# Small transfers, the last modulation sum and the modulation itself rearranged in a two-layer decoder trunk

## What is computed

```python
cond = jax.nn.silu(c)
mod = (cond @ ada_w[layer] + ada_b[layer])[:, None, :]
sh_m, sc_m, g_m, sh_f, sc_f, g_f = jnp.split(mod, 6, axis=-1)
h = _rmsnorm(x, gn[0]) * (1.0 + sc_m) + sh_m
...
x = x + g_m * _rmsnorm(y, gn[1])
h = _rmsnorm(x, gn[2]) * (1.0 + sc_f) + sh_f
```

## Time and profile before

| | us |
|---|---|
| median of three runs | 901.51 (900.4 to 906.21) |
| profiled execution, its own time | 900.82 |
| its span (first to last instruction) | 899.3 |
| TensorE busy | 837.3 (93%) |
| VectorE busy | 705.9 (78%) |
| ScalarE busy | 524.3 (58%) |
| mean granted TensorE clock | 0.972 of full |

### The profile page before, as it was taken

How to read it: one execution, slowest core, us unless ns; L and a number is a source line. 1 busy time by engine, 2 the same in 40 slices (tenths; PEclk the granted TensorE clock), 3 DMA queues, 4 the chain that set the end, 5 groups by cost and what they waited for, 6 DMA issues and landing times.

```text
span 899.3 us, 12482 instructions
## 1 busy us (share of the span) xinstructions
PE 837.3 (93%) x4720; PEld 741.3 (82%) x4720; DVE 705.9 (78%) x585; ACT 524.3 (58%) x531; POOL 37.9 (4%) x46
## 2 busy tenths in 40 slices
PE   2999999899999999988798899999999999999993
PEld 2999777899999888877677788888888888888882
DVE  4888677876666988553855988898988889898977
ACT  2224924444444434334545678787979787878873
POOL 1001001000000101010000300000000000000120
PEclk9899999899999999689999999999999999999998
DMA  9989867297778998379912799999999999999991
GB/s 341 410 306 377 302 253 286 97 353 262 268 271 300 368 344 322 117 264 420 390 47 61 254 396 343 422 359 419 360 408 360 408 365 406 385 386 393 368 373 47
DMA packets 46239, 283.52 MB, mean 315 GB/s; under 512 B 5855, under 2 KB 5858, under 8 KB 19834
## 3 DMA queue, kind: packets, MB, share of 16 engines
q1 hardware_dynamic: 41002, 268.80, 77.7%
q0 software_dynamic: 3312, 12.06, 3.3%
q10 hardware_dynamic: 1888, 2.15, 0.7%
HBM read 257.82 MB, written 25.17 MB: 315 GB/s over the span
## 4 chain that ended last, share of the span: by engine, by line
PE 81%; DVE 12%; ACT 2%; DMA 2%; issue 2%; ACTq 1%; DVEq 0%; SPq 0%
PE ps L1712 9%; PE ps L1713 9%; PE ps L1717 9%; PE ps L1358 6%; PE ps L1360 6%; PE ps L1361 6%; PE ps L1320 5%; PE ps L1322 5%; PE ps L1321 5%; PE ps L1735 4%; PE ps L1729 4%; PE ps L1730 4%; DVE acc L853 3%; DVE w_lo L837 2%; PE ps L1380 2%; DMA ring<-in_moe_w_down 2%
## 5 line engine op out<-in xcount | busy, mean ns | idle before, releaser
L1169 DVE TENSOR_TENSOR w_lo<-ring,w_hi 128x2048 fp32r<-128x2048 f32 (+1 forms) x96 | 209.7, 2202 | 38.1 <-ACT w_hi L733 36.8
L515 ACT ACTIVATE w_hi<-ring 128x2048 fp32r<-128x2048 f32 (+2 forms) x58 | 109.7, 1893 | 198.0 <-PE ps L1361 100.6
L837 DVE TENSOR_TENSOR w_lo<-ring,w_hi 128x2048 fp32r<-128x2048 f32 (+2 forms) x58 | 138.3, 2385 | 77.1 <-ACT w_hi L515 77.1
L733 ACT ACTIVATE w_hi<-ring 128x2048 fp32r<-128x2048 f32 (+1 forms) x96 | 175.7, 1839 | 20.4 <-PE ps L1717 11.9
L1358 PE MATMUL ps<-hT_lo,w_hi 128*128 128x256 f32 x480 | 137.8, 287 | 4.6 <-DVE hT_lo L876 2.4
L1360 PE MATMUL ps<-hT_hi,w_hi 128*128 128x256 f32 x480 | 136.7, 285 | 0.0
L1361 PE MATMUL ps<-hT_hi,w_lo 128*128 128x256 f32 x480 | 136.7, 285 | 0.0
L853 DVE SCALAR_TENSOR_TENSOR acc<-ring,cond,acc 128x2048 f32<-128x2048 f32 x42 | 98.7, 2349 | 2.7
L1712 PE MATMUL ps<-w_hi,xe_hi 128*128 128x512 f32 (+1 forms) x256 | 97.7, 382 | 2.5 <-DVE xe_lo L1243 2.5
L1358 PEld LDWEIGHTS ps<-hT_lo,w_hi 128*128 128x128 f32 x480 | 93.2, 194 | 5.7 <-issue 2.8
L1169 DVE TENSOR_TENSOR m_lo<-ring,m_hi 128x2048 fp32r<-128x2048 f32 (+2 forms) x48 | 92.7, 1932 | 6.3 <-ACT m_hi L733 6.3
(11 more groups left out here) (289 smaller groups left out, 1442.2 us busy)
## 6 DMA issues: line engine op xcount, KB each, us to landing
ring<-in_moe_w_gu SPq DMA_DIRECT2D x64, 1024.0 KB, 7.1
ring<-in_ada_w SPq DMA_DIRECT2D x48, 1024.0 KB, 6.9
ring<-in_moe_w_down SPq DMA_DIRECT2D x40, 1024.0 KB, 8.3
ring<-in_moe_w_gu SPq DMA_DIRECT2D x32, 768.0 KB, 8.9
ring<-in_ffn_w_gu SPq DMA_DIRECT2D x22, 1024.0 KB, 5.0
ring<-in_sb_w_in SPq DMA_DIRECT2D x12, 1024.0 KB, 7.5
ring<-in_ffn_w_down SPq DMA_DIRECT2D x11, 1024.0 KB, 6.1
x_rows<-blank SPq DMA_DIRECT2D x1, 8704.0 KB, 27.1
```

Of the source, the lines that this page charges most:

```text
L515: act.activation(w_hi[m % 2][:, 0:cols_n], ring[n % R][:, 0:cols_n], ACT.Copy).then_inc(hi_done, 1)
L733: act.activation(m_hi[k % NB][:, 0:n_c], ring[(N0 + k) % R][:, 0:n_c], ACT.Copy).then_inc(hi_done, 1)
L837: dve.tensor_tensor(w_lo[m % 2][:, 0:cols_n], ring[n % R][:, 0:cols_n], w_hi[m % 2][:, 0:cols_n].bitcast(F32), ALU.subtract).then_inc(free ...
L1169: dve.tensor_tensor(m_lo[k % NB][:, 0:n_c], ring[(N0 + k) % R][:, 0:n_c], m_hi[k % NB][:, 0:n_c].bitcast(F32), ALU.subtract).then_inc(free ...
```

## The change

Four edits, the diff below cut to its core.

1. ScalarE issues `wr`, `br` and the three bias rows no longer ahead of its first computation, but after the first `xhat`. `pos_i` stays, and counts in `s_lat` instead of `s_small`.
2. The first `xhat` is made by ScalarE (Copy with a scale) instead of VectorE, and VectorE's two reciprocals for it stand behind three `ada_w` pieces instead of two.
3. The last of the first eight `ada_w` pieces is added in two halves. TensorE sums the first half (shift) when `ada_half` is up, does three dummy matmuls, then waits for the second (scale).
4. In all three modulations ScalarE computes pairs 1 and 2 of `t32` (Identity with scale and bias), VectorE pairs 0 and 3. In the first one ScalarE does this ahead of `hi(1)`.

```diff
@@ scalar
             act.dma_start(pos_i[:, :], pos_d[0].rearrange("(c p) -> p c", p=P),
-                          allow_slow_non_contiguous=True).then_inc(s_small, 16)
-            act.dma_start(wr[:, :, :], w_router[0].rearrange("(k p) n -> p k n", p=P)).then_inc(s_small, 16)
-            act.dma_start(br[:, :], b_router).then_inc(s_small, 16)
...
-                act.dma_start(rows[32 * n:32 * n + 1, :], ada_b_rows[row:row + 1]).then_inc(s_bias, 16)
-
+                          allow_slow_non_contiguous=True).then_inc(s_lat, 16)
...
-            def modulated_hi(v):
+            def modulated_hi(v, b0=0):
+                def modulate(b):
+                    act.wait_ge(tr_done, 4 * v + b + 1)
+                    act.wait_ge(mod_ok, v + 1)
+                    for k in (2 * b, 2 * b + 1):
+                        ins = act.activation(t32[:, k, :], ps[:, b0 + b, (k % 2) * T:(k % 2 + 1) * T], ACT.Identity,
+                                             scale=scale[:, v, k:k + 1], bias=shift[:, v, k:k + 1])
+                    ins.then_inc(t_act, 1)
+
+                modulate(1)
                 for b in range(4):
-                    act.wait_ge(t_done, 4 * v + b + 1)
+                    if b == 2:
+                        modulate(2)
+                    if b in (0, 3):
+                        act.wait_ge(t_done, 2 * v + b // 3 + 1)
+                    else:
+                        act.wait_ge(t_act, 2 * v + b)
                     act.activation(hT_hi[:, 2 * b:2 * b + 2, :], t32[:, 2 * b:2 * b + 2, :], ACT.Copy)\
                         .then_inc(hThi, 1)
...
             for c in range(TC):
                 root(0, c)
+            for c in range(TC):
+                act.wait_ge(rstd_done, c + 1)
+                act.activation(xhat[:, c, :], x[:, c, :], ACT.Copy, scale=rstd[:, 0, c:c + 1]).then_inc(xhat_done, 1)
+            act.dma_start(wr[:, :, :], w_router[0].rearrange("(k p) n -> p k n", p=P)).then_inc(s_small, 16)
+            act.dma_start(br[:, :], b_router).then_inc(s_small, 16)
...
+                act.dma_start(rows[32 * n:32 * n + 1, :], ada_b_rows[row:row + 1]).then_inc(s_bias, 16)
             hi(0)
+            modulated_hi(0)
             hi(1)
-            modulated_hi(0)
@@ vector
-                for b in range(4):
+                for b in (0, 3):
                     dve.wait_ge(tr_done, 4 * v + b + 1)
...
                     ins.then_inc(t_done, 1)
-                    if b:
-                        cut(b - 1)
+                    if b == 0:
+                        cut(0)
+                        cut(1)
+                cut(2)
                 cut(3)
...
-            ada(2)
-            normalise(0)
-            ada(DC - 2)
+            ada(3)
+            for c in range(TC):
+                inverse_root(0, c)
+            ada(DC - 4)
+            n = pieces[0]
+            pieces[0] += 1
+            wait_piece(dve, n)
+            dve.wait_ge(freed, n)
+            for a, done in ((0, ada_half), (1, freed)):
+                half = slice(a * D, (a + 1) * D)
+                dve.scalar_tensor_tensor(acc[:, half], ring[n % R][:, half], cond[:, n:n + 1], acc[:, half], ALU.mult,
+                                         ALU.add).then_inc(done, 1)
             lo(0)
@@ tensor
             for k in range(3, DC):
                 pe.wait_ge(freed, k)
                 keep_clock(9)
+            pe.wait_ge(ada_half, 1)
+            mod_columns(0, 4, (0,))
+            keep_clock(3)
             ada_ready(0, 0)
-            mod_columns(0, 4)
+            mod_columns(0, 4, (1,))
             keep_clock(8)
```

More of the change, by code:

```diff
@@ L300, in trunk @@
         cols_ok = sem("cols_ok")
-        cond_ok = sem("cond_ok")
+        cond_ok, ada_half = sem("cond_ok"), sem("ada_half")
         mod_mm, mod_ok = sem("mod_mm"), sem("mod_ok")
@@ L309, in trunk @@
         tr_done = sem("tr_done")
-        t_done, hThi, hTlo = sem("t_done"), sem("hThi"), sem("hTlo")
+        t_done, t_act, hThi, hTlo = sem("t_done"), sem("t_act"), sem("hThi"), sem("hTlo")
         ev_qkv, v_c0 = sem("ev_qkv"), sem("v_c0")
@@ L576, in _ @@
                 root(0, c)
+            for c in range(TC):
[3 more added lines that the diff above has]
+            act.dma_start(br[:, :], b_router).then_inc(s_small, 16)
+            ada_b_rows = ada_b.rearrange("l (s n) -> (l s) n", s=6)
+            for n in (1, 2, 3):
+                l, w = gates[n]
+                row = 6 * l + 3 * w + 2
+                act.dma_start(rows[32 * n:32 * n + 1, :], ada_b_rows[row:row + 1]).then_inc(s_bias, 16)
             hi(0)
+            modulated_hi(0)
             hi(1)
-            modulated_hi(0)
             def flat(g):
@@ L634, in _ @@
             hi(M + 5)
-            modulated_hi(1)
+            modulated_hi(1, 4)
             M = first["gu"]
@@ L662, in _ @@
             hi(M + 1)
-            modulated_hi(2)
+            modulated_hi(2, 4)
             hi(M + 2)
@@ L865, in normalise @@
             def normalise(u, halves=range(TC)):
-                if u == 0:
-                    dve.wait_ge(s_x, 16)
                 for c in halves:
@@ L946, in _ @@
             dve.tensor_copy(lat_g[:, :], ps[:, 6, HR:HR + 3])
-            dve.wait_ge(s_small, 48)
+            dve.wait_ge(s_lat, 64)
             link(dve.tensor_copy(pos_f[:, :], pos_i[:, :]))
@@ L1049, in _ @@
             mod_cols(3, 3)
+            dve.wait_ge(s_small, 32)
             dve.tensor_tensor(wr_mod[:, :, :], wr[:, :, :], scale[:, 3, :].unsqueeze(2).broadcast_to([P, DC, E]), ALU.mult)\
@@ L1374, in transpose_xhat, with mod_columns @@
                             ins.then_inc(tr_done, 1)
-            def mod_columns(v, b):
+            def mod_columns(v, b, parts=range(2)):
                 l, w = divmod(v, 2)
-                for s in range(2):
+                for s in parts:
                     for k in range(DC):
@@ L1382, in mod_columns @@
                                         ones[:, 0:1], start=True, stop=True)
-                ins.then_inc(mod_mm, 1)
+                if s == 1:
+                    ins.then_inc(mod_mm, 1)
             def gate_spread(n, b0):
@@ L1427, in _ @@
                 if g == 0:
-                    pe.wait_ge(s_lat, 48)
+                    pe.wait_ge(s_lat, 64)
                     pe.matmul(ps[:, 6, 0:HR], ones[0:1, :], freq[0:1, :], start=True, stop=True)
@@ L1553, in _ @@
             ins.then_inc(lat_T, 1)
-            pe.wait_ge(s_small, 48)
+            pe.wait_ge(s_small, 32)
             for k in range(DC):
```

4 lines of the change are left out of this document (removed).

## The result

| us | before | changed |
|---|---|---|
| median of 18 runs each, taken side by side | 902.59 (897.6 to 908.71) | 898.23 (892.19 to 900.72) |
| ratio, 95% interval | | 0.9935 (0.991 to 0.996) |
| profiled execution: own time, span, mean granted clock | 900.82, 899.3, 0.972 | 900.58, 898.0, 0.972 |

The ratio of runs taken side by side makes it a gain of 5.9 us (3.6 to 8.1); the two medians differ by 4.4. By the bound of 1% the result still counts as no change.

What follows compares the result with a forecast made beforehand. It took TensorE, with 81% of the chain of waits, to bound the kernel. Its terms, +1.5 for the start, -0.5 and +0.2 for the second and third modulation, added +1.2 us to the profiled 900.82: 902.0, range 898.5 to 904.5.

Steps and rivals of the forecast that it cites:

- Parts 1 to 3: Start: `cond` 3.1 us earlier, last piece 2.0 earlier, transposes 1.64 later; gapless dummy bursts to 33.82 absorb VectorE's gain.
- The delay that I gave the sums: Start: bursts behind the later transposes end at 33.82, so the column sums start 1.16 us later than 32.66.
- The rival in which TensorE's queue doesn't bind: Start: VectorE's gain comes through, second product 3.3 us earlier, total 897.2; chance 12%.
- Part 4: First column sums and products: the clock falls among the sums, the second product starts at 48.9, not 47.37; +1.5 us.
- the clock holds: Rival at the first sums: clock falls only 4.9 us after they begin, start costs 0, total 900.5; chance 30%.
- I count 1.3 us gained: First modulation: VectorE's low part for the second product gains 1.3 us from sharing, but is covered, ending at 48.2.
- Part 5: Modulation shared with ScalarE, about 1.0 us per pair: second modulation -0.5 us (bounds -0.6 and 0), third +0.2.
- The third: Third modulation: TensorE waits only for the first low part, no second wait to save; +0.2 us (0 to +0.6).

Runs made afterwards that it cites:

- e3: Changed kernel with three bursts of nine dummy matmuls instead of five ahead of the first column sums; 894.07 us, ratio to before 0.9884.
- e1: Kernel before with only the ScalarE sharing in all three modulations, `hi(1)` behind the first; 898.75 us, ratio 0.9922.
- e5: Kernel before with the second modulation alone shared with ScalarE; 898.38 us, ratio 0.9941.
- e6: Kernel before with the third modulation alone shared with ScalarE; 904.69 us, ratio 1.0006.
- e8: Kernel before, nothing shared, with six more dummies behind the transposes of the second and third modulation; 898.49 us, ratio 0.9953.
- e2: Changed kernel without the sharing, so the rebuilt start alone; 904.2 us, ratio to before 0.9981.
- e4: Changed kernel once more, unchanged, for a second profile; 894.59 us, ratio to before 0.9914.
- e9: Changed kernel with six more dummies behind the transposes of the second and third modulation; 898.27 us, ratio to before 0.9955.
- e10: Changed kernel with three start bursts, six dummies added twice, and the third round's second column sums moved into a later wait; 885.02 us, ratio to before 0.9834.
- e7: Kernel before with the first modulation alone shared with ScalarE, `hi(1)` behind it; 901.43 us, ratio 0.9972.

## Why the prediction was wrong

**Parts 1 to 3 held**: `cond` at 9.0, the last half near 30.0 (forecast 30.65), `xhat` at 18.6 and 19.7 (18.9, 19.9), bursts without a gap to 33.32 (33.82). The delay that I gave the sums is hardly there, though: they start at 32.66 to 33.39 in the eight profiles with the old start and at 32.85 to 33.45 in the four with the new start and five bursts. The rival in which TensorE's queue doesn't bind is refuted by e3.

**Part 4 failed, and turned the sign of the start.** Its step was "down at 36.95", and then "with the clock back 6.8 us after its fall, at 43.75", which gave +1.5. In the profile after, the clock fell at 38.15, 1.2 us later, and was back 3.4 us after that. I had taken both from "this very place", but it was the place in another program. With the old start (eight profiles) the clock fell 1.9 to 4.1 us after the sums began and stayed down 6.8 us in five of them (before, e1, e5, e6, e8), 3.4 in three. With the new one, sums in two parts and dummies between, it fell 3.9 to 4.8 us after in all five in which it fell (changed, e2, e3, e4, e9), was back after 3.4 each time, and in e10 didn't fall. So the rival "the clock holds", with its "the dummies between the halves help" and 0 for this stage, was the better reading, though the clock did fall. Whether the dummies between did it, or something else of the new start, was not tried. Measured, the start alone gives +0.3 ± 0.4 at equal clock.

**With it went the first modulation's gain.** The text had its size nearly, "I count 1.3 us gained" (1.28 from the kernel before to e7, 1.0 against the six other profiles), and then booked it as covered, because the slow first product of Part 4 ended later still, at 48.9. The product ended at 46.9, level with the low part, so the gain was on the path: -1.1 in e7. It was priced at zero behind a cover that rested on that reading of the clock.

**Part 5, the second modulation, was mis-sized**: -0.5 (bounds -0.6 and 0) for a measured -2.6 ± 0.6 at equal clock. The prices of its instructions were right: ScalarE's pair 1.02 us (forecast 1.0) beside VectorE's 0.99, and the wait of 0.47 went. The Trainium skill's rule ("ScalarE: Activation LUTs", "Rules for kernel authors") that multiplies and adds belong on VectorE is not borne out by these rows, float32 read from PSUM. What the sum left out is the step behind, half clock in the next product: 1.5 us where it is avoided, but that sharing avoids it is not clear of chance. Most of the rest stays open. The third, +0.2 forecast, gave -0.6 ± 0.5.

**What no term had** is the change of the mean clock itself, 2.0 of the 6.5 us between the mean spans.

**The basis.** The sum stood on one execution, whose mean clock of 0.972 was above the 0.969 of 67 runs. With three runs shown (900.40 to 906.21), a spread of several us was to be seen; the range took its width from the steps alone. Its lower end, 898.5, missed by 0.3.

What stays open: about 2 us of the second modulation at equal clock, and why the changed kernel's clock is higher, by 0.003 (2.0 us by the line), and in e4 by 0.0062 over its set. Each half of the change may raise it alone (e1 by 0.0025, e2 by 0.0027 over the same set, each ± 0.0015); the shorter time at half clock in the new start would be one part of that.

## What to carry to other kernels

When an engine keeps itself busy with work nobody reads, count that work as a queue: an upstream gain stops there until the filler is cut (e3). A gain that is "covered" deserves its full price in the range if the cover ends within a microsecond or two of it, above all if the cover's length depends on the clock. And where runs differ by their clock, compare kernels on the line of span against clock before reading steps of 1 us, and don't take the clock's pattern in one profile for the kernel's. When profiles differ, mark the same instructions in each: here that showed two long stages that never vary, and so where to look.

## What the runs showed of the hardware

- TensorE counts as fully busy in one-column sums (1.00 of 1.00 us in the window of 35 to 36 of the earlier trace rows), and yet its clock falls 1.9 to 4.9 us after they begin (start and second round of all profiles that show a fall there). In the third round 32 of them took 6.83 us at half clock in ten profiles, 4.04 in e1, and 3.63 at full clock in e3, e9 and e10. At the start of e10, where the sums began at 29.80, the windows show no fall at all; in e3, where they began at 29.54, they do.
- The same program has its stretches at half clock in other places from run to run. For the kernel before, the mean clock ranges over 0.962 to 0.981 and the span over 892.5 to 906.6 us. The Trainium skill ("TensorE: Matmul & The Clock Gate", "What's actually happening") calls the number of slow matmuls variable from run to run; these runs agree, with 14 us of 900 at stake.
- ScalarE modulates 128x256 float32 from PSUM about as fast as VectorE (1.02 and 0.99 us for two).
- Small transfers can stand long in the issuing engine: `br` took 5.43 us on ScalarE's sequencer right behind `wr` in the kernel before; issued near 18 us in the changed kernel, the two took 0.39 and 0.44 us.
